# Modulation sums of the second block moved into the first block's feed-forwards

## The reference, cut to what matters

```python
u = causal_dwconv(h @ w_up, conv_w, conv_b)          # w_up: 1024 x 5632
ua, ub = _split(u, (FFN_DIM, FFN_DIM))                # FFN_DIM = 2816
x = x + rmsnorm((jax.nn.gelu(ua) * ub) @ w_down, norm_ffn_post)
```

```python
cond_lat, cond_ctx = jax.nn.silu(c), jax.nn.silu(c_ctx)
mod  = (cond_lat @ ada_w[i] + ada_b[i])               # ada_w[i]: 1024 x 6144
modc = (cond_ctx @ ada_w[i] + ada_b[i])
sh1, sc1, g1, sh2, sc2, g2 = jnp.split(mod, 6, axis=-1)
h = modulate(rmsnorm_2(x, norm1_g[i]), sh1, sc1)      # then attention, gates g1, g2, feed-forward
```

## Time and profile before

| | |
|---|---|
| Median of 3 runs | 5363.23 us (5355.7 to 5368.65) |
| The profiled execution | 5369.66 us |
| Span of its trace | 5368.2 us |
| PE busy | 4653.3 us (87%) |
| DVE busy | 2125.2 us (40%) |
| ACT busy | 1504.8 us (28%) |
| POOL busy | 646.5 us (12%) |
| Bytes moved by DMA | 351.65 MB, 66 GB/s over the span |
| Mean granted TensorE clock | 0.915 of full speed |

### The profile page before, as it was taken

How to read it: one execution, slowest core, us unless ns; L and a number is a source line. 1 busy time by engine, 2 the same in 40 slices (tenths; PEclk the granted TensorE clock), 3 DMA queues, 4 the chain that set the end, 5 groups by cost and what they waited for, 6 DMA issues and landing times. The chain is left out here.

```text
span 5368.2 us, 75318 instructions
## 1 busy us (share of the span) xinstructions
PE 4653.3 (87%) x32814; PEld 3523.3 (66%) x32814; DVE 2125.2 (40%) x3061; ACT 1504.8 (28%) x2596; POOL 646.5 (12%) x459
## 2 busy tenths in 40 slices
PE   6797997799877997979899688888889999779899
PEld 4684884587655865937587426565668885447687
DVE  3536433456345346333553412336332230334323
ACT  2523231333224232312333212135221120213222
POOL 1215100011012033000110100101000000023000
PEclk9898897899989997979999889789889999879999
DMA  3131002122221320012122151000011114300222
GB/s 129 36 110 43 4 19 80 61 90 91 83 80 40 102 75 6 4 64 90 63 94 91 52 188 52 24 31 1 32 44 63 63 58 159 98 16 29 74 98 83
DMA packets 95880, 351.65 MB, mean 66 GB/s; under 512 B 9920, under 2 KB 11328, under 8 KB 94400
## 3 DMA queue, kind: packets, MB, share of 16 engines
q1 hardware_dynamic: 85824, 312.51, 17.6%
q10 hardware_dynamic: 9728, 34.32, 1.7%
HBM read 332.11 MB, written 14.68 MB: 65 GB/s over the span
## 5 line engine op out<-in xcount | busy, mean ns | idle before, releaser
L285 DVE TENSOR_TENSOR wlo<-ring,whi 128x1024 fp32r<-128x1024 f32 x494 | 605.0, 1225 | 1988.3 <-ACT whi L275 1988.1
L275 ACT CAST whi<-ring 128x1024 fp32r<-128x1024 f32 x494 | 517.6, 1048 | 2410.3 <-PE ps L325 2229.1
L322 PE MATMUL ps<-h_hi,whi 128*128 128x512 f32 x1552 | 621.7, 401 | 98.4 <-DVEq L223 36.6
L325 PE MATMUL ps<-h_hi,wlo 128*128 128x512 f32 x1552 | 611.8, 394 | 0.0
L323 PE MATMUL ps<-h_lo,whi 128*128 128x512 f32 x1552 | 610.5, 393 | 0.0
L322 PE MATMUL ps<-hm_hi,whi 128*128 128x512 f32 (+1 forms) x1408 | 506.2, 359 | 105.1 <-POOL spread L1730 66.0
L323 PE MATMUL ps<-hm_lo,whi 128*128 128x512 f32 (+1 forms) x1408 | 478.8, 356 | 0.0
L325 PE MATMUL ps<-hm_hi,wlo 128*128 128x512 f32 (+1 forms) x1408 | 420.2, 356 | 0.0
L322 PEld LDWEIGHTS ps<-h_hi,whi 128*128 128x128 f32 x1552 | 295.9, 191 | 171.4 <-issue 52.3
L322 PEld LDWEIGHTS ps<-hm_hi,whi 128*128 128x128 f32 x1408 | 268.0, 190 | 184.2 <-POOL spread L1730 66.8
L322 PE MATMUL ps<-ac_hi,whi 128*128 128x512 f32 x880 | 328.5, 373 | 28.0 <-DVE ac_lo L450 24.8
(11 more groups left out here) (356 smaller groups left out, 7868.5 us busy)
## 6 DMA issues: line engine op xcount, KB each, us to landing
ring<-in_w SPq DMA_DIRECT2D x596, 512.0 KB, 3.3
x_spill<-x ACTq DMA_DIRECT2D x2, 2048.0 KB, 7.2
h_spill<-h ACTq DMA_DIRECT2D x2, 2048.0 KB, 6.3
m_spill<-m ACTq DMA_DIRECT2D x2, 2048.0 KB, 8.4
h<-h_spill ACTq DMA_DIRECT2D x2, 2048.0 KB, 7.7
ma<-m_spill ACTq DMA_DIRECT2D x2, 2048.0 KB, 8.1
x<-x_spill ACTq DMA_DIRECT2D x2, 2048.0 KB, 13.1
x<-in_x ACTq DMA_DIRECT2D x1, 2048.0 KB, 15.8
```

Source lines behind the costliest of these rows:

```text
L275: self.A.copy(self.hi[k % 2][:], raw).then_inc(self.s_cut_hi.h, 1)
L285: self.V.tensor_tensor(self.lo[k % 2][:], raw, self.hi[k % 2][:].bitcast(F32), ALU.subtract).then_inc(self.s_cut_lo.h, 1)
L322: T.matmul(ps[:, b, 0:cw], hi, xh(q, c0, cw), start=q == 0, stop=False, skip_group_check=True)
L325: m = T.matmul(ps[:, b, 0:cw], lo, xh(q, c0, cw), start=False, stop=q == kt - 1, skip_group_check=True)
```

## The change

The 12 rows of 8 matmuls of each modulation are made in the feed-forward of the first block's layer of the same number. `modulation_sums` takes 16 blocks of outputs at a time (3 rounds a = 0, 1, 2 for the 48 blocks) and 8 tiles of the contraction (k), so 24 steps i. A step has 4 matmuls g = 0 to 3: all with the same stationary `cond[:, k, :]`, which now is 128 x 32 (two condition vectors and 30 columns of zeros), each with another raw 128 x 512 slice, and each writing to its own 32 partitions 32g to 32g+31 of bank 4 or 5. Step i stands behind column 2i + 1 of the up stage (22 steps), the last two behind columns 0 and 1 of the down stage. After a round ACT copies the whole 128 x 512 bank to `mrow`, four matmuls turn it with the constant `rows8` (128 x 8), and DVE puts the result into `mod_sums`. `modulation` keeps only the DVE operations (bias and gains) between its two fences.

With it go: two raw pieces of ada_w behind every second cut piece of the up weights, and two behind the third and the sixth piece of the down weights; two counters of tiles, one for cut and one for raw; a DMA of `cond` (128 KB) among the loads at the start, where Silu is now applied as well; and the `cond` columns leave `par2`. The matmuls' number is the same, 96 of 512 columns for each layer; the turns are 12 matmuls for each layer in place of 48.

```diff
 HYBRID = [(80, "cut"), (16, "cut"), (128, "cut"), (24, "cut"), (192, "cut"), (8, "raw"), (16, "raw"), (128, "cut"),
-          (64, "cut"), (16 * FT, "cut"), (8 * FT, "cut"), (80, "cut")]
-DIFF = [(384, "raw"), (128, "cut"), (64, "cut"), (64, "cut"), (16 * FT, "cut"), (8 * FT, "cut")]
-GQA = [(384, "raw"), (80, "cut"), (16, "cut"), (64, "cut"), (16 * FT, "cut"), (8 * FT, "cut")]
+          (64, "cut"), *[(16, "cut"), (16, "raw")] * FT, *[(24, "cut"), (16, "raw")] * 2, (128, "cut"), (80, "cut")]
+DIFF = [(128, "cut"), (64, "cut"), (64, "cut"), (16 * FT, "cut"), (8 * FT, "cut")]
+GQA = [(80, "cut"), (16, "cut"), (64, "cut"), (16 * FT, "cut"), (8 * FT, "cut")]
...
+    def modulation_sums(self, layer):
+        T, V, A, ps = self.T, self.V, self.A, self.ps
+        row = [self.view(f"mrow{i}", 42000 + 512 * i, 512) for i in range(2)]
+        steps = self.plan_raw(24 * 4, 4)
+        b_row, b_back, b_mods = self.s_mrow.take(3), self.s_mback.take(3), self.s_mods.take(3)
+
+        def pe(i):
+            a, k = divmod(i, DT)
+            if i == 0:
+                T.wait_ge(self.s_cond.h, 1)
+            if k == 0 and a == 2:
+                T.wait_ge(self.s_mrow.h, b_row + 1)
+            for g in range(4):
+                T.matmul(ps[32 * g:32 * g + 32, 4 + a % 2, :], self.cond[:, k, :], self.raw_of(steps[4 * i + g]),
+                         start=k == 0, stop=k == DT - 1, skip_group_check=True).then_inc(self.s_raw.h, 1)
+
+        def pe_back(a):
+            T.wait_ge(self.s_mrow.h, b_row + a + 1)
+            if a > 0:
+                T.wait_ge(self.s_mods.h, b_mods + a)
+            for q in range(4):
+                m = T.matmul(ps[:, 6, 8 * q:8 * q + 8], row[a % 2][:, q * P:(q + 1) * P], self.c("rows8", 8), start=True,
+                             stop=True, skip_group_check=True)
+            m.then_inc(self.s_mback.h, 1)
+
+        def act(a):
+            A.wait_ge(self.s_raw.h, steps[4 * (DT * a + DT - 1) + 3].value)
+            if a == 2:
+                A.wait_ge(self.s_mback.h, b_back + 1)
+            A.copy(row[a % 2][:], ps[:, 4 + a % 2, :]).then_inc(self.s_mrow.h, 1)
...
-    def conv_ffn(self):
+    def conv_ffn(self, layer):
...
+        def pe_tick(n):
+            if n % 2:
+                mod_pe(n // 2)
+            if n in (18, 34):
+                mod_back(n // 16 - 1)
+
         def act_tick(n, value):
             q, h = divmod(n, 2)
+            if n in (16, 32):
+                mod_act(n // 16 - 1)
...
+            if n in (20, 36):
+                mod_dve(n // 16 - 1)
...
+        def down_pe_tick(n):
+            if n < 2:
+                mod_pe(2 * FT // 2 + n)
+            if n == 3:
+                mod_back(2)
...
     def modulation(self, layer):
-        T, V, A, ps = self.T, self.V, self.A, self.ps
+        V = self.V
         self.fence()
...
-            for n in range(12):
-                if n >= 2:
-                    T.wait_ge(self.s_mrow.h, b_row + n - 1)
-                for q in range(DT):
-                    T.matmul(ps[0:2, n % 2, :], condv[:, q, :], self.raw_of(steps[DT * n + q]), start=q == 0,
-                             stop=q == DT - 1, skip_group_check=True).then_inc(self.s_raw.h, 1)
-                if n > 0:
-                    pe_back(n - 1)
...
+        A.dma_start(self.cond[:], self.a["cond"]).then_inc(self.s_load.h, 16)
+        e = self.s_load.take(80) + 80
...
+        A.activation(self.cond[:], self.cond[:], ACT.Silu).then_inc(self.s_cond.h, 1)
```

More of the change, by code:

```diff
@@ L62 @@
 for _n, _w in (("ada_b", 96), ("norm1", 16), ("norm2", 16), ("dq", 1), ("dk", 1), ("gq", 1), ("gk", 1),
-               ("subln", 1), ("lam", 4), ("cond", 16)):
+               ("subln", 1), ("lam", 4)):
     COLS2[_n] = _at
@@ L144, in __init__ @@
         self.par = nc.alloc_sbuf_tensor("par", [P, max(NC1, NC2)], F32)
-        self.sml = nc.alloc_sbuf_tensor("sml", [P, 640], F32)
+        self.sml = nc.alloc_sbuf_tensor("sml", [P, 320], F32)
+        self.mod_sums = nc.alloc_sbuf_tensor("mod_sums", [P, 2, 48, 2], F32)
+        self.cond = nc.alloc_sbuf_tensor("cond", [P, DT, 32], F32)
         self.big = nc.alloc_sbuf_tensor("big", [P, BIG], F32)
@@ L174, in __init__ @@
                     self.piece_of.append(p)
-        self.tile = 0
+        self.raw_pieces = [p for p, kind in enumerate(self.kinds) if kind == "raw"]
+        self.cut_tile = self.raw_tile = 0
         self.cut_end = {}
@@ L236, in plan @@
         for i in range(n_steps):
-            p, at = divmod(self.tile, PIECE)
-            k = self.cut_of[p]
+            k, at = divmod(self.cut_tile, PIECE)
+            p = self.piece_of[k]
             steps.append(Step(p, k, at, width, at == 0, base + i + 1))
@@ L242, in plan @@
                 self.release[p] = (self.s_cut_lo, k + 1)
-            self.tile += width
+            self.cut_tile += width
         return steps
@@ L249, in plan_raw @@
         for i in range(n_steps):
-            p, at = divmod(self.tile, PIECE)
-            assert self.cut_of[p] is None
+            r, at = divmod(self.raw_tile, PIECE)
+            p = self.raw_pieces[r]
             steps.append(Step(p, None, at, width, at == 0, base + i + 1))
@@ L254, in plan_raw @@
                 self.release[p] = (self.s_raw, base + i + 1)
-            self.tile += width
+            self.raw_tile += width
         return steps
@@ L562, in hybrid @@
         self.mix_and_project()
-        self.conv_ffn()
+        self.conv_ffn(layer)
         self.layer_embedding(layer)
@@ L1468, in mix_and_project, with dve @@
                      ready=lambda j: A.wait_ge(self.s_xadd.h, b_add + j + 1))
-    def conv_ffn(self):
+    def modulation_sums(self, layer):
[25 more added lines that the diff above has]
+            A.copy(row[a % 2][:], ps[:, 4 + a % 2, :]).then_inc(self.s_mrow.h, 1)
+        def dve(a):
+            V.wait_ge(self.s_mback.h, b_back + a + 1)
+            out = self.mod_sums[:, layer, 16 * a:16 * a + 16, :].rearrange("p (g q) c -> p q g c", q=4)
+            V.tensor_copy(out, ps[:, 6, 0:32].rearrange("p (q g c) -> p q g c", q=4, g=4)).then_inc(self.s_mods.h, 1)
+        return pe, pe_back, act, dve
+    def conv_ffn(self, layer):
         T, V, A, G, ps = self.T, self.V, self.A, self.G, self.ps
@@ L1480, in conv_ffn @@
         zeroed = self.s_vq.n
+        mod_pe, mod_back, mod_act, mod_dve = self.modulation_sums(layer)
         cols = self.columns(2 * FT, DT)
@@ L1523, in conv_ffn @@
         go(*self.dense(cols, lambda q, c0, cw: h_hi[:, q, c0:c0 + cw], lambda q, c0, cw: h_lo[:, q, c0:c0 + cw], SEG1,
-                       lambda n: [n % 4], free, act_tick=act_tick, dve_tick=dve_tick, pool_tick=pool_tick))
+                       lambda n: [n % 4], free, None, pe_tick, act_tick, dve_tick, pool_tick))
         self.fence()
@@ L1534, in free, with down_act_tick, down_dve_tick @@
                 T.wait_ge(self.s_z.h, b_z + n - 3)
-        def act_tick(n, value):
+        def down_pe_tick(n):
[3 more added lines that the diff above has]
+                mod_back(2)
+        def down_act_tick(n, value):
             A.wait_ge(self.s_mm.h, value)
             A.copy(ZF[:, n, :], ps[:, n % 4, :]).then_inc(self.s_z.h, 1)
+            if n == 2:
+                mod_act(2)
+        def down_dve_tick(n, value):
+            if n == 4:
+                mod_dve(2)
         go(*self.dense(cols, lambda q, c0, cw: a_hi[:, q, c0:c0 + cw], lambda q, c0, cw: a_lo[:, q, c0:c0 + cw], SEG1,
-                       lambda n: [n % 4], free, lambda q: T.wait_ge(self.s_hlo.h, b_half + q + 1), act_tick=act_tick))
+                       lambda n: [n % 4], free, lambda q: T.wait_ge(self.s_hlo.h, b_half + q + 1), down_pe_tick,
+                       down_act_tick, down_dve_tick))
         self.down_done = cols[-1][-1].value
@@ L1657, in act @@
[L1657 to L1668, removed]
-            self.vdone()
[L1670 to L1677, removed]
@@ L1678, in modulation @@
-        go(pe(), act(), dve())
+        b = self.p2("ada_b", 48 * layer, 48).unsqueeze(2).to_broadcast([P, 48, 2])
+        self.vq(V.tensor_tensor(self.mods, self.mod_sums[:, layer, :, :], b, ALU.add))
+        self.vdone()
+        for which, norm in ((0, "norm1"), (1, "norm2")):
+            g = self.p2(norm, 8 * layer, 8).unsqueeze(2).to_broadcast([P, 8, 2])
+            sc = self.mods[:, 24 * which + 8:24 * which + 16, :]
+            o = self.gs[:, 16 * which:16 * which + 16].rearrange("p (j c) -> p j c", c=2)
+            self.vq(V.tensor_scalar(o, sc, 1.0, None, ALU.add))
+            self.vdone()
+            self.vq(V.tensor_tensor(o, o, g, ALU.mult))
@@ L2239, in start @@
         G.wait_ge(self.s_load.h, e)
+        A.activation(self.cond[:], self.cond[:], ACT.Silu).then_inc(self.s_cond.h, 1)
+        self.s_cond.take(1)
         ang, nn, r_ = (self.view(n, A1 + i * S, S)[:] for i, n in enumerate(("ang", "turns", "rest")))
@@ L2280, in whole @@
         G.wait_ge(self.s_par.h, e)
```

(23 more changed lines are left out.)

9 lines of the change are left out of this document (1 added, 8 removed).

## The result

The changed kernel takes 5288.65 us (median; 5286.42 to 5292.24) against 5364.86 us before: a ratio of 0.9858, 95% interval [0.9846, 0.9871]. That is 76 us less. The forecast was 134 us less (5230, range 5222 to 5272), so the direction came out, and some 58 us of the gain are missing.

The account below looks back on a forecast made before the run. It took TensorE, busy 4653 of 5368 us, to bound the kernel. 193.2 us removed against 59.9 added (52.9 + 6.6 + 0.4) gave 133.3 less: 5236.4 for the profiled execution, 5230 as median, range 5222 to 5272.

Parts of the forecast that it names:

- What is removed: In the two modulations: norms start 97.9 and 95.3 us earlier, 193.2 us in all off the end of the kernel.
- What a set costs: Four matmuls on four column groups between ordinary matmuls: 0.86 us streaming plus 0.29 us changing over and back, 1.15 us.
- Full overlap of four: In a set, all four matmuls run together on their column groups, giving 5230 us; chance 0.68.
- two at a time: Rival: only two column groups overlap in a set, 2.01 us each, 5270 us; chance 0.18 shared with the page's loss factor.
- the Trainium skill's factor for packed tiles: Four row tiles gave 3.07 times, so a set streams 0.26 us longer, about 5242 us; chance 0.18 shared with two at a time.
- no overlap: Rival: a set's four matmuls run one behind another, 3.73 us a set, 118.7 us over forecast, 5349 us; chance 0.08.
- The turns: Turning each round's sums on TensorE, 3 for each layer: 1.1 us each, 6.6 us for all 6.
- How many are on the path: Of 48 sets in both layers, 46 cost TensorE time, 52.9 us; one in each layer is hidden.
- the seam's cover: Behind the last up column TensorE idles 7.42 us, hiding one set in each layer; failure would cost 2.3 us more.
- Ring, clock: Up stage: weight pieces land in time and the clock stays 1.00, costing nothing; rival of a dry ring, chance 0.06.
- Start: Initial loads: 128 KB more cost 0.4 us; Silu and its table load lie under DVE's work and cost nothing.
- records of a set that start one by one: Sign of a wrong forecast in TensorE's timeline, meaning two at a time or no overlap; right was two groups of four.

## Why the prediction was wrong

One step was missing from the sum, and the large ones held. The step that failed is the treatment of everything outside the change as unchanged: the prediction went through the queues that the change passes, and said of the start only that its loads cost 0.4 us. It did not ask what the new tensors do to the addresses of the old ones. They moved `big` by 32 bytes against the weights' halves (modulo 256), and ordinary matmuls of 512 columns then start every 233.0 ns in place of 228.4. That term stood at nothing without a reason, and it is worth 5288.65 - 5234.69 = 54.0 us. With `big` where it was, the change comes to 5234.69 us, 4.7 us above the forecast.

- *What is removed* (193.2 us): measured 97.9 and 95.3 in the changed kernel.
- *What a set costs* (1.15 us): 1.19 in the changed kernel, 1.20 with `big` at its old address. Full overlap of four was the likeliest case, and it held; neither loss by two at a time nor the Trainium skill's factor for packed tiles ("TensorE: Matmul & The Clock Gate", "Part 3: Packing small matmuls — row/col tiling"), by which the prediction estimated 0.26 us more, showed. The surcharge for no overlap, 2.58 us a set, was measured as 2.57.
- *The turns* (1.1 us each): 0.90.
- *How many are on the path* (46): right, the seam's cover held.
- *Ring, clock*: no wait of TensorE for weights in the first up stage, though ACT waits; granted clock 1.00 there from 9 us after its start, that is 2.4 GHz.
- *Start* (+0.4 us): sign wrong. The start of Silu loads ACT's table under the first loads, and the sine that follows needs no load of its own. Where ACT loaded a table at 25.39 us before, it now goes on at once, worth 1.3 us against 0.3 for the later loads:

```profile
13.69 1.28 ACT L2269 ACT_TABLE_LOAD   x1 [13.69 <-issue]
...
25.64 0.63 ACT L2295 ACTIVATE tab<-rest 128x512 f32<-128x512 f32 x1 [4.59 <-DVE rest L2293]
```

The forecast sum, 133.3 us, stands against 133.0 between the spans of the kernel before and of the version with `big` at its old address, and against 131.3 between the medians of the same set of runs (5366.02 and 5234.69). That it is so near is in part luck: in that version the two layers with the sets took 32.1 and 33.0 us more, where the forecast had 29.8 each, and the rest of the second block came out 3.9 us and the start 1.4 us shorter than forecast. Where these few us lie was not traced. The prediction's sign for a wrong forecast, records of a set that start one by one, was never seen with four groups; what was seen, a slower step of ordinary matmuls ahead of any set, was not on its list.

What stays open is why the step depends on the distance. The halves are loaded while the last matmul still streams from `big`: PEld is busy for 202.8 and PE for 275.7 of the same 278 us of the first up stage. That the two readings collide in memory is a guess; it was not isolated from other explanations, and a collision would have to spare the matmuls of 256 columns, which have as many weight loads and did not slow down. Nor was it tried whether the pattern repeats at exactly 256 bytes: shown is only that places 512 bytes apart are alike (within 0.3 us of the change's worth), twice. A pattern that repeats at 512 bytes would fit all these runs as well.

## What to carry to other kernels

A change that allocates, grows or drops a tensor moves whatever is allocated behind it; where matmuls run back to back, first compare the step between two ordinary matmuls in a stage that the change does not touch, and pin the operands' addresses before judging the change. And small-output matmuls on separate groups of columns, spread over a stage that TensorE bounds, cost one matmul's stream and about 0.3 us for four.

## What the runs showed of the hardware that was not expected

An unused tensor of 32 bytes made the kernel 1.1% slower, and the same 32 bytes ahead of both operands made no difference [0.9988, 1.0006]. With moving operand and weights' halves at a distance of 0 modulo 256 bytes the fp32r matmuls of 512 columns step at 228.3 ns on average; at 32, at 233.0. One distance does not mean one step, though. By start times in the first up stage, the step in the changed kernel alternates between 231 and 236 ns, changing over behind each set and each turn; in the kernel before with `big` 32 bytes up, which has no sets there, it is 231.1 ns throughout; at distance 0 it is 228.9 ns with and without sets. So at distance 32 the sets seem to bear on the pace too, by some 2 us a stage; why is open as well.

In a set the passes do not run matmul by matmul: by the start times of its records, the first passes of all four start within 0.02 us, and the four second passes 0.45 us later. With all four on one group of columns a first and a second pass take turns, 0.43 us apart. Whether the order differs already in TensorE's queue, the traces do not say.
